# A chain of feed-forward and mixing layers on one core: the last group of the 512-token layers written out, with other buffers for activations and squares

## The chip, the cores and the metric

The kernel runs on one core of one Trainium2 chip. Its engines are TensorE (matmuls, PE in the profile), VectorE (DVE), ScalarE (ACT), GpSimd (POOL) and SyncE (SP), which issues most of the DMAs. The metric is the device time of one execution in microseconds; the kernel before has a median of 2832.19 us over 3 runs (2831.08 to 2836.46). A program order is given to each engine by hand, and engines wait for one another by semaphores; there is no scheduler.

## The reference, cut to what matters

The model has two blocks of two layers each over 256 tokens of width 1024; the first block also carries 256 context tokens along. Around every mixer (pooling, differential attention, a recurrent mixer, a dilated attention) stand gated feed-forward steps. All is in float32.

```python
def rms_norm(x, g):
    xf = x.astype(jnp.float32)
    y = xf * lax.rsqrt(jnp.mean(xf * xf, axis=-1, keepdims=True) + NORM_EPS)
    return (y * g.astype(jnp.float32)).astype(x.dtype)

def swiglu(h, w_in, w_out):
    g, u = jnp.split(h @ w_in, 2, axis=-1)
    return (jax.nn.silu(g) * u) @ w_out

def ffn_step(s, g, shift, scale, gate, w_in, w_out):
    return s + 0.5 * gate * swiglu(modulate(rms_norm(s, g), shift, scale), w_in, w_out)
...
x = ffn_step(x, ...)      # ffn 0 and, for layer 1, ffn 2: 256 tokens x and 256 tokens xc
x = x + mx[5] * ox        # ox: pooling in layer 0, attention in layer 1
x = ffn_step(x, ...)      # ffn 1 (with xc) and ffn 3 (x alone)
```

The hidden width is 2816, in 11 groups of 256. In the first block the modulation (`shift`, `scale`, `gate`) comes from two vectors times `ada_w`.

## The kernel before

**Layout.** Features lie on the partitions, tokens along a row: `x` is 128 x 8 x 512 (`KT` = 8 feature tiles; tokens 0 to 255 are `x`, 256 to 511 the context, `HALVES`). A matmul of two float32 operands is done as three (`mm3`): weights and activations are split into a high part (`whi`, `hh`, `ah`) and a low rest (`wlo`, `hl`, `al`). ScalarE makes each high part (`split_hi`), VectorE each low part (`split_lo`). Weights come in chunks of 1 MB into three slots of `wraw`; chunk n is split when the matmuls of chunk n - 3 are done.

**A feed-forward layer** (`ffn`, one such function for each engine). ffn 0, 1 and 2 have 512 tokens, ffn 3 to 7 have 256. For each of 11 groups: gate products into `ps_g`, up products into `ps_u`, ScalarE's silu into `sg`, VectorE's product into `tmp`, then the high part into `ah` (ScalarE, `hidden`) and the low rest into `al` (VectorE, `hidden`). TensorE's down products of a group run one group late: gate i+1, up i+1, down i. A down product has eight tiles, each in one of four PSUM banks `ps_o`; VectorE adds each into `x` (`residual`: two additions of 256 columns for 512 tokens) and thereby frees its bank (`o_free`). After the loop the down products of the last group follow at once. There is one `ah`/`al` for all groups. With 256 tokens the last iteration stands written out, and its activations go to the free half of the buffer (`last_hi`, `last_lo`), with VectorE's two splits placed among the tiles. With 512 tokens all ten iterations are in the loop. In ffn 0 to 2 VectorE also computes the modulation (`ada_block`, 3 or 4 a group, on rows loaded by GpSimd's queue), lines 1475 and 1478.

**A norm** (`norm`). ScalarE squares each tile of `x` after its last addition (line 765), GpSimd adds the first `POOLED[k]` squares up (line 668), TensorE multiplies the rest and the pooled sum with ones into `ps_g` (`pooled_sums`, line 2253), ScalarE takes roots (lines 784 and 786), VectorE the reciprocal (1296, 1291), and then each tile is scaled (VectorE, 1314), shifted into `hh` (ScalarE, 806) and its rest put in `hl` (VectorE, 1327), tokens 0 to 255 first. TensorE runs matmuls nobody reads meanwhile (`keep_clock`, 2237). The norms are numbered k: k = 1 stands between ffn 0 and the pool mixer, 2 ahead of ffn 1, 3 ahead of ffn 2, 4 ahead of the attention, k = 5 and on have 256 tokens. For k = 1 the whole 512 columns are handled in one piece, for 2 to 4 by halves from the root on.

**Late chunks.** The split of the chunk after the next two is put off to the end of the norm (`late`); for k = 4 `early=True` puts it ahead of the root and the reciprocal. There it is the chunk of the attention's v weights, the third of `qkv`. TensorE first makes two tiles of q and two of k (`diff_first`), then v tiles, each of which waits for the bank two tiles back. VectorE copies the q and k tiles out in order, behind the lambda arithmetic (lines 1778 to 1783).

## Time and profile before

| | us |
|---|---|
| median of 3 runs | 2832.19 |
| profiled execution, its own time | 2833.92 |
| its span | 2832.3 |
| TensorE busy | 2725.0 |
| VectorE busy | 2049.1 |
| ScalarE busy | 1011.9 |
| GpSimd busy | 139.6 |
| granted TensorE clock, mean | 0.981 |

A busy share says how long an engine had an instruction in it, not whether the end waited for it. A time line row gives start and duration in us, then engine, line and operation, with the idle time ahead of it and what ended it in brackets. Matmuls overlap: their pace is the distance of starts, not the duration shown. A line number is that of the kernel before.

### The profile page before, as it was taken

To read this page: it belongs to the slowest core of one execution; us is meant where nothing else is said; L and a number is where in the kernel's file an instruction comes from. 1 tells how busy PE (TensorE), PEld (TensorE's weight loads), DVE (VectorE), ACT (ScalarE), POOL (GpSimd) and SP (SyncE) were. 2 spreads that over 40 slices of the span, in tenths; PEclk is the share of its full clock that TensorE was granted. 3 is DMA by queue.
4 is the path that set the end of the run, shared out by engine and by line. 5 is a ranking of instruction groups with operands and counts; after the bars stand their busy time and mean duration, and the time that the engine had idled before them with its cause. 6 is when DMAs were issued, how large, how long until landed. Compare 5 with 4: busy or idle time off the path is not lost.

```text
span 2832.3 us, 49047 instructions
## 1 busy us (share of the span) xinstructions
PE 2725.0 (96%) x19250; PEld 2418.7 (85%) x19250; DVE 2049.1 (72%) x3067; ACT 1011.9 (36%) x1167; POOL 139.6 (5%) x204
## 2 busy tenths in 40 slices
PE   6999999999999999999999999998899999999999
PEld 4888878788878888788799899977799989986999
DVE  5877778766777777776676766756767776665677
ACT  4222234222232222333344444553144434443534
POOL 1000011000010000100000000000000010000000
PEclk9999999999999999999999999999999999997999
DMA  8444432533334444322245344521044554443344
GB/s 348 163 174 168 161 150 70 180 136 133 133 124 159 153 180 164 132 90 75 86 176 193 136 178 178 188 86 62 3 169 178 193 142 178 188 168 67 119 185 186
DMA packets 68705, 421.43 MB, mean 149 GB/s; under 512 B 7672, under 2 KB 8824, under 8 KB 26592
## 3 DMA queue, kind: packets, MB, share of 16 engines
q1 hardware_dynamic: 48176, 343.36, 32.8%
q0 software_dynamic: 20432, 76.69, 8.4%
q8 instruction: 71, 1.16, 0.2%
q14 instruction: 26, 0.21, 0.0%
HBM read 418.95 MB, written 1.07 MB: 148 GB/s over the span
## 4 chain that ended last, share of the span: by engine, by line
PE 84%; DVE 9%; issue 3%; ACT 2%; DMA 1%; POOL 1%; SPq 0%; DVEq 0%; ACTq 0%; POOLq 0%
PE ps_o L2230 11%; PE ps_o L2232 10%; PE ps_o L2231 10%; PE ps_g L2230 7%; PE ps_u L2230 7%; PE ps_u L2232 7%; PE ps_u L2231 7%; PE ps_g L2232 7%; PE ps_g L2231 7%; DVE wlo L1261 2%; PE ps_o L2469 1%; DMA scr<-in_AW 1%; DVE tsq L1314 1%; PE ps_g L2253 1%; DVE scr L1475 1%
## 5 line engine op out<-in xcount | busy, mean ns | idle before, releaser
L761 ACT ACTIVATE whi<-wraw 128x2048 fp32r<-128x2048 f32 x314 | 598.8, 1911 | 788.5 <-PE ps_u L2232 371.2
L1261 DVE TENSOR_TENSOR wlo<-wraw,whi 128x2048 fp32r<-128x2048 f32 x314 | 712.3, 2290 | 163.8 <-ACT whi L761 163.7
L2230 PE MATMUL ps_g<-hh,wlo 128*128 128x256 f32 (+1 forms) x1464 | 464.1, 317 | 6.4 <-DVE hl L1327 3.9
L2230 PE MATMUL ps_o<-ah,wlo 128*128 128x256 f32 (+1 forms) x1408 | 454.8, 323 | 15.5 <-DVE x L1367 7.9
L2230 PE MATMUL ps_u<-hh,wlo 128*128 128x256 f32 (+1 forms) x1464 | 462.5, 316 | 0.0
L2232 PE MATMUL ps_g<-hh,whi 128*128 128x256 f32 (+1 forms) x1464 | 462.1, 316 | 0.0
L2231 PE MATMUL ps_g<-hl,whi 128*128 128x256 f32 (+1 forms) x1464 | 462.1, 316 | 0.0
L2232 PE MATMUL ps_u<-hh,whi 128*128 128x256 f32 (+1 forms) x1464 | 462.1, 316 | 0.0
L2231 PE MATMUL ps_u<-hl,whi 128*128 128x256 f32 (+1 forms) x1464 | 461.9, 316 | 0.0
L2231 PE MATMUL ps_o<-al,whi 128*128 128x256 f32 (+1 forms) x1408 | 453.0, 322 | 0.0
L2232 PE MATMUL ps_o<-ah,whi 128*128 128x256 f32 (+1 forms) x1408 | 452.8, 322 | 0.0
L1367 DVE SCALAR_TENSOR_TENSOR x<-ps_o,gcol,x 128x256 f32<-128x256 f32 x640 | 281.9, 479 | 126.7 <-PE ps_o L2232 121.0
L2230 PEld LDWEIGHTS ps_g<-hh,wlo 128*128 128x128 f32 x1464 | 275.9, 188 | 29.6 <-issue 10.6
L2230 PEld LDWEIGHTS ps_o<-ah,wlo 128*128 128x128 f32 x1408 | 265.6, 189 | 40.3 <-issue 8.8
L2231 PEld LDWEIGHTS ps_g<-hl,whi 128*128 128x128 f32 x1464 | 275.9, 188 | 18.6
L2230 PEld LDWEIGHTS ps_u<-hh,wlo 128*128 128x128 f32 x1464 | 275.7, 188 | 18.9 <-issue 0.2
L2232 PEld LDWEIGHTS ps_g<-hh,whi 128*128 128x128 f32 x1464 | 275.8, 188 | 18.7
L2231 PEld LDWEIGHTS ps_u<-hl,whi 128*128 128x128 f32 x1464 | 275.7, 188 | 18.7
L2232 PEld LDWEIGHTS ps_u<-hh,whi 128*128 128x128 f32 x1464 | 275.7, 188 | 18.7
L2232 PEld LDWEIGHTS ps_o<-ah,whi 128*128 128x128 f32 x1408 | 265.8, 189 | 21.1
L2231 PEld LDWEIGHTS ps_o<-al,whi 128*128 128x128 f32 x1408 | 265.6, 189 | 20.8
L880 ACT ACTIVATE ah<-tsq 128x512 fp32r<-128x512 f32 (+1 forms) x88 | 69.8, 793 | 463.0 <-PE ps_o L2232 447.0
(461 smaller groups left out, 3677.0 us busy)
## 6 DMA issues: line engine op xcount, KB each, us to landing
wraw<-in_W SPq DMA_DIRECT2D x315, 1024.0 KB, 4.8
...
x<-in_XT SPq DMA_DIRECT2D x1, 2048.0 KB, 10.3
...
```

The lines of the kernel that those rows point to most:

```text
L761: nc.scalar.activation(whi[:, n % SLOTS, :], wraw[:, n % SLOTS, :], ACT.Copy).then_inc(w_hi, 1)
L880: nc.scalar.activation(dst[:, :, 0:N], tmp[:, :, 0:N], ACT.Copy).then_inc(a_hi, 1)
L1261: tt_(wlo[:, n % SLOTS, :], wraw[:, n % SLOTS, :], whi[:, n % SLOTS, :].bitcast(f32), sub).then_inc(w_lo, 1)
L1314: stt(dst, src(d)[:, HALVES[j]], A(d, j), rstd[:, HALVES[j]], mult, mult).then_inc(nm_t, 1)
L1367: ins = stt(x[:, d, HALVES[j]], src[:, HALVES[j]], gate(d, j), x[:, d, HALVES[j]], mult, add)
L1475: stt(ada_junk[:, 0, :], ada_w[:, slot, :], 1.0, ada_c[:, 0, :], mult, mult, accum_out=mod_col(b, 0, i, per)).then_inc(ad_left, 1)
L2230: mm(out, a[1], b[0], start=first, stop=False)
L2231: mm(out, a[0], b[1], start=False, stop=False)
L2232: return mm(out, a[0], b[0], start=False, stop=last)
L2253: ins = mm(out, ones, tsq[:, d * NTOK:d * NTOK + N], start=d == order[0], stop=d == order[-1])
L2469: ins = mm(att_out(g)[unit["rows"]], unit["v"][b], probs_t[a][g % 2][:, b, :], start=b == 0, stop=b == nb - 1)
```

## The change

The last iteration of the loop is written out for 512 tokens as well, on ScalarE and VectorE. Its activations go to new buffers `th` and `tl`, which lie in the second half of `tsq`; the squares 4 to 7 of the norms after these layers (k = 1, 3, 4: `AFTER_WIDE`) go to `hid` instead. For k = 2, 3, 4 (`SUM_HALVES`) each sum of squares is made of two matmuls of 256 columns in two banks, and the first half has a semaphore step of its own. `POOLED` is 5 in place of 6 for k = 1, 3, 4, and the pooled sum is taken as the last but one. The early split of k = 4 is gone. In the written-out iteration, for 256 tokens too, the second split stands behind two tiles of the last group instead of three.

```diff
 LATE = (5, 7)
-POOLED = {1: 6, 2: 6, 3: 6, 4: 6, 5: 4, 6: 4, 7: 3, 8: 6, 9: 6, 10: 6, 11: 6, 12: 6}
+SUM_HALVES = (2, 3, 4)
+AFTER_WIDE = (1, 3, 4)
+POOLED = {1: 5, 2: 6, 3: 5, 4: 5, 5: 4, 6: 4, 7: 3, 8: 6, 9: 6, 10: 6, 11: 6, 12: 6}
...
         x = sb("x", [128, KT, NTOK])
+        with nc.sbuf_tensor("off_t", [128, KT * NTOK // 2], f32), nc.sbuf_tensor("th", [128, 2, NTOK], f32r) as th, nc.sbuf_tensor("tl", [128, 2, NTOK], f32r) as tl:
+            pass
...
         wide, narrow = (hh, hl, ah, al), (hh2, hl2, ah2, al2)
-        last_hi, last_lo = ah2[:, :, NX:NTOK], al2[:, :, NX:NTOK]
+        last = {NX: (ah2[:, :, NX:NTOK], al2[:, :, NX:NTOK]), NTOK: (th, tl)}
...
             return [(b0 + q, s, fills[s] + slots[:q + 1].count(s)) for q, s in enumerate(slots)], fills
+        def squared_at(k, d, N):
+
+            return cut(hid, (d - KT // 2) * NTOK, N) if k in AFTER_WIDE and d >= KT // 2 else cut(tsq, d * NTOK, N)
+
+        def summed(k, part=1):
+
+            return k + sum(q < k for q in SUM_HALVES) + 1 + (part if k in SUM_HALVES else 0)
+
...
         HN_MEM = [ps_o[:, 3, :], BANK[3]]
-        ffn_loop = lambda N: GROUPS - 2 if N == NX else GROUPS - 1
+        ffn_loop = GROUPS - 2
...
                         pool.wait_ge(nm_acc, pooled(k) + d - 1)
-                    nt(tsq[:, 0:N], tsq[:, 0:N], tsq[:, d * NTOK:d * NTOK + N], add).then_inc(nm_acc, 1)
+                    nt(tsq[:, 0:N], tsq[:, 0:N], squared_at(k, d, N), add).then_inc(nm_acc, 1)
...
                 nc.scalar.activation(whi[:, n % SLOTS, :], wraw[:, n % SLOTS, :], ACT.Copy).then_inc(w_hi, 1)
-            def square(src, N, ready, d):
+            def square(src, N, ready, d, k=0):
                 ready(act, d)
-                nc.scalar.activation(tsq[:, d * NTOK:d * NTOK + N], src(d)[:, 0:N], ACT.Square).then_inc(nm_sq, 1)
+                nc.scalar.activation(squared_at(k, d, N), src(d)[:, 0:N], ACT.Square).then_inc(nm_sq, 1)
...
                     for d in range(squared, KT):
-                        square(src, N, ready, d)
+                        square(src, N, ready, d, k)
                         memory_out(memory, 0)
-                    act.wait_ge(nm_sum, k + 1)
+                    act.wait_ge(nm_sum, summed(k, 0))
                     rest = HALVES[1] if by_half else slice(0, N)
-                    nc.scalar.activation(rstd[:, rest], ps_g[:, 0, rest], ACT.Sqrt, bias=C("eps", 1), scale=1.0 / D).then_inc(nm_std, 1)
+                    act.wait_ge(nm_sum, summed(k))
+                    nc.scalar.activation(rstd[:, rest], ps_g[:, 1, 0:NX] if k in SUM_HALVES else ps_g[:, 0, rest], ACT.Sqrt, bias=C("eps", 1), scale=1.0 / D).then_inc(nm_std, 1)
...
                     split_hi(n0 + 7, i, step, per)
-                if N == NX:
-                    i = GROUPS - 2
-                    if f not in LATE:
-                        split_hi(n0 + 5, i, step, per)
-                    silu(i * step + DONE[n0 + 2], i + (g0 + 1), i + (lg + 2))
-                    if f in LATE:
-                        split_hi(n0 + 5, i, step, per)
-                    nc.scalar.activation(cols[:, 61:62], C("eps", 1), ACT.Sqrt)
-                    hidden(i + (g0 + 1), last_hi)
-                    split_hi(n0 + 6, i, step, per)
-                    split_hi(n0 + 7, i, step, per)
+                i = GROUPS - 2
+                if f not in LATE:
+                    split_hi(n0 + 5, i, step, per)
+                silu(i * step + DONE[n0 + 2], i + (g0 + 1), i + (lg + 2))
+                if f in LATE:
+                    split_hi(n0 + 5, i, step, per)
+                nc.scalar.activation(cols[:, 61:62], C("eps", 1), ACT.Sqrt)
+                hidden(i + (g0 + 1), last[N][0])
+                split_hi(n0 + 6, i, step, per)
+                split_hi(n0 + 7, i, step, per)
...
             ffn(2, NTOK)
-            norm(lambda d: x[:, d, :], NTOK, mod(1, 1), "split", after(FIRST["qkv", 0]), FIRST["qkv", 0], part=3, early=True)
+            norm(lambda d: x[:, d, :], NTOK, mod(1, 1), "split", after(FIRST["qkv", 0]), FIRST["qkv", 0], part=3)
...
                     split_lo(n_down + SLOTS, i, per)
-                if N == NX:
-                    i = GROUPS - 2
-                    done = i * step + DONE[n_down - 1]
-                    if f in LATE:
-                        scale_gate(i * step + DONE[n0 + 2], i + (g0 + 1))
-                        scale_silu(i + (g0 + 1))
+                i = GROUPS - 2
+                done = i * step + DONE[n_down - 1]
+                for s in range(per_ada):
+                    if s == 2:
+                        split_lo(n0 + 5, i, per)
+                    ada_block(b0 + s, s, 16 * (fills[s] + 1), i, per_ada)
+                if f in LATE:
+                    scale_gate(i * step + DONE[n0 + 2], i + (g0 + 1))
+                    scale_silu(i + (g0 + 1))
+                if per_ada < 3:
                     split_lo(n0 + 5, i, per)
-                    product(i + (g0 + 1), i * step + DONE[n_up], i + (lg + 2))
-                    down(n_down, done, range(1))
-                    hidden(i + (g0 + 1), last_hi, last_lo)
-                    down(n_down, done, range(1, 4))
-                    split_lo(n_up + SLOTS, i, per)
-                    down(n_down, done, range(4, KT))
-                    down(n_last, DONE[n_last - 1], range(3))
-                    split_lo(n_down + SLOTS, i, per)
-                    down(n_last, DONE[n_last - 1], range(3, KT))
-                else:
-                    down(n_last, DONE[n_last - 1])
+                product(i + (g0 + 1), i * step + DONE[n_up], i + (lg + 2))
+                down(n_down, done, range(1))
+                hidden(i + (g0 + 1), *last[N])
+                down(n_down, done, range(1, 4))
+                split_lo(n_up + SLOTS, i, per)
+                down(n_down, done, range(4, KT))
+                down(n_last, DONE[n_last - 1], range(2))
+                split_lo(n_down + SLOTS, i, per)
+                down(n_last, DONE[n_last - 1], range(2, KT))
...
             ffn(2, NTOK, gate(1, 0))
-            norm(xs_, NTOK, A_mod(1, 1), B_mod(1, 1), "split", part=3, early=True)
+            norm(xs_, NTOK, A_mod(1, 1), B_mod(1, 1), "split", part=3)
...
             def pooled_sums(out, k, N):
-                order = [0] + list(range(POOLED[k], KT))
-                if POOLED[k] == 4:
-                    order = [4, 5, 6, 0, 7]
-                elif POOLED[k] < 6:
+                order = [*range(POOLED[k], KT - 1), 0, KT - 1] if k < 7 else [0, *range(POOLED[k], KT)]
+                if k == 7:
                         pe.wait_ge(nm_sq, k * KT + d + 1)
-                    ins = mm(out, ones, tsq[:, d * NTOK:d * NTOK + N], start=d == order[0], stop=d == order[-1])
-                ins.then_inc(nm_sum, 1)
+                    if k in SUM_HALVES:
+                        for j, half in enumerate(HALVES):
+                            ins = mm(ps_g[:, j, 0:NX], ones, squared_at(k, d, N)[:, half], start=d == order[0], stop=d == order[-1])
+                            if d == order[-1]:
+                                ins.then_inc(nm_sum, 1)
+                    else:
+                        ins = mm(out, ones, squared_at(k, d, N), start=d == order[0], stop=d == order[-1])
+                if k not in SUM_HALVES:
+                    ins.then_inc(nm_sum, 1)
...
                     down(n_down, i * tiles + TILE0[n_down], i + g0, i)
-                down(n_last, TILE0[n_last], g0 + GROUPS - 1, last=f < 7, a=(last_hi, last_lo) if N == NX else (ah, al))
+                down(n_last, TILE0[n_last], g0 + GROUPS - 1, last=f < 7, a=last[N])
```

The helper for a source's place, and the number of steps of the sums' semaphore, are `squared_at` and `summed` above. What moves on three engines follows, before and after apart.

VectorE, end of ffn 0: from the loop's branch, before (`mods` and `acol` are modulation arithmetic):

```order
L1399 TENSOR_TENSOR al<-tsq,ah 128x1024
L1260 REGISTER_ALU
L1261 TENSOR_TENSOR wlo<-wraw,whi 128x2048
L1260 REGISTER_ALU
L1261 TENSOR_TENSOR wlo<-wraw,whi 128x2048
L1427 REGISTER_ALU
L1427 COMPARE_AND_BRANCH
L1367 SCALAR_TENSOR_TENSOR x<-ps_o,gcol,x 128x256 x16
L1527 TENSOR_TENSOR mods<-mods,vec 128x40 x2
```

The same place after, from the product of the last written-out group:

```order
L1407 TENSOR_TENSOR tsq<-tsq,ps_u 128x1024
L1379 SCALAR_TENSOR_TENSOR x<-ps_o,gcol,x 128x256 x2
L1411 TENSOR_TENSOR tl<-tsq,th 128x1024
L1379 SCALAR_TENSOR_TENSOR x<-ps_o,gcol,x 128x256 x6
L1273 TENSOR_TENSOR wlo<-wraw,whi 128x2048
L1379 SCALAR_TENSOR_TENSOR x<-ps_o,gcol,x 128x256 x12
L1273 TENSOR_TENSOR wlo<-wraw,whi 128x2048
L1379 SCALAR_TENSOR_TENSOR x<-ps_o,gcol,x 128x256 x12
L1541 TENSOR_TENSOR mods<-mods,vec 128x40 x2
```

The low rest comes behind one tile of the last but one group (two additions a tile), one split behind four tiles, the other behind two tiles of the last group.

TensorE, end of ffn 1 and the sums of squares of k = 3, before (`cst` holds the ones, `ps_u` is written by `keep_clock`):

```order
L2230 MATMUL ps_o<-ah,wlo 128x512
L2231 MATMUL ps_o<-al,whi 128x512
L2232 MATMUL ps_o<-ah,whi 128x512
L2253 MATMUL ps_g<-tsq,cst 128x512 x3
L2237 MATMUL ps_u<-cst 128x512 x4
```

And after:

```order
L2244 MATMUL ps_o<-th,wlo 128x512
L2245 MATMUL ps_o<-tl,whi 128x512
L2246 MATMUL ps_o<-th,whi 128x512
L2267 MATMUL ps_g<-hid,cst 128x256 x4
L2267 MATMUL ps_g<-tsq,cst 128x256 x2
L2267 MATMUL ps_g<-hid,cst 128x256 x2
L2251 MATMUL ps_u<-cst 128x512 x4
```

Three sums of 512 columns become eight of 256: squares 5 and 6, the pooled sum, square 7.

VectorE, end of the norm ahead of the attention, before (`hl` is the norm's last step, `lamb` the lambda arithmetic, `scr<-ps_o` the copies of q and k):

```order
L1327 SCALAR_TENSOR_TENSOR hl<-tsq,mods,hh 128x256 x2
L1778 TENSOR_TENSOR lamb<-lamb 128x64 x2
L1779 TENSOR_REDUCE cols<-lamb 128x2
L1781 TENSOR_TENSOR cols<-cols 128x1
L1782 TENSOR_SCALAR cols<-cols 128x1
L1783 TENSOR_SCALAR cols<-vec 128x1
L1662 TENSOR_SCALAR scr<-ps_o 128x256 x2
L1664 COPY scr<-ps_o 128x512 x2
```

And after:

```order
L1339 SCALAR_TENSOR_TENSOR hl<-tsq,mods,hh 128x256 x2
L1273 TENSOR_TENSOR wlo<-wraw,whi 128x2048
L1792 TENSOR_TENSOR lamb<-lamb 128x64 x2
L1793 TENSOR_REDUCE cols<-lamb 128x2
L1795 TENSOR_TENSOR cols<-cols 128x1
L1796 TENSOR_SCALAR cols<-cols 128x1
L1797 TENSOR_SCALAR cols<-vec 128x1
L1676 TENSOR_SCALAR scr<-ps_o 128x256 x2
L1678 COPY scr<-ps_o 128x512 x2
```

The split of the v weights stands ahead of the lambda arithmetic and of all copies; ScalarE's half of it moves behind the last tile of the norm in the same way.

## Rows read from the trace of the kernel before

**Rows 1.** The page: busy time, share of the span and instructions of TensorE.

```profile
PE 2725.0 (96%) x19250; PEld 2418.7 (85%) x19250; DVE 2049.1 (72%) x3067; ACT 1011.9 (36%) x1167; POOL 139.6 (5%) x204
```

**Rows 2.** Time line of TensorE, end of ffn 0: start, duration, instruction, idle before.

```profile
396.35 0.59 PE L2230 MATMUL ps_o<-ah,wlo 128*128 128x512 f32 x1 [2.53 <-issue]
...
408.70 0.39 PE L2232 MATMUL ps_o<-ah,whi 128*128 128x512 f32 x1
410.06 2.84 PE L2253 MATMUL ps_g<-tsq,cst 128*128 128x512 f32 x6 [0.97 <-POOL tsq L668]
```

**Rows 3.** Time line of ScalarE, end of ffn 0.

```profile
393.93 1.06 ACT L880 ACTIVATE ah<-tsq 128x1024 fp32r<-128x1024 f32 x1 [9.04 <-PE ps_o L2232]
...
410.04 0.63 ACT L765 ACTIVATE tsq<-x 128x512 f32<-128x512 f32 x1 [0.73 <-DVE x L1367]
```

**Rows 4.** Time line of VectorE, end of ffn 0.

```profile
383.15 1.22 DVE L1395 TENSOR_TENSOR tsq<-tsq,ps_u 128x1024 f32<-128x1024 f32 x1 [2.24 <-PE ps_u L2232]
...
393.85 0.88 DVE L1367 SCALAR_TENSOR_TENSOR x<-ps_o,gcol,x 128x256 f32<-128x256 f32 x2 [0.48 <-PE ps_o L2232]
395.02 1.23 DVE L1399 TENSOR_TENSOR al<-tsq,ah 128x1024 fp32r<-128x1024 f32 x1 [0.29 <-ACT ah L880]
396.16 4.48 DVE L1261 TENSOR_TENSOR wlo<-wraw,whi 128x2048 fp32r<-128x2048 f32 x2
```

**Rows 5.** Time line of GpSimd, end of ffn 0.

```profile
402.97 7.04 POOL L668 TENSOR_TENSOR tsq<-tsq 128x512 f32<-128x512 f32 x5 [15.97 <-ACT tsq L765]
```

**Rows 6.** Stretches: length, busy TensorE (x), loads, DVE, ACT, POOL; granted clock, DMA.

```profile
396.35:400.06 3.71, 3.71 (x9) 2.91 (x10) 3.71 (x2) 1.93 (x3) 0.00 (x0) 0.54 0.32 89
1182.40:1186.00 3.60, 3.60 (x16) 2.97 (x17) 3.60 (x2) 1.92 (x3) 0.00 (x0) 1.00 0.15 27
```

**Rows 7.** Time lines of ScalarE and VectorE, ends of ffn 1 and ffn 2.

```profile
806.96 1.06 ACT L880 ACTIVATE ah<-tsq 128x1024 fp32r<-128x1024 f32 x1 [9.04 <-PE ps_o L2232]
...
826.53 1.75 DVE L1296 RECIPROCAL rstd<-rstd 128x256 f32<-128x256 f32 x1 [2.86 <-ACT rstd L784]
...
1179.97 1.06 ACT L880 ACTIVATE ah<-tsq 128x1024 fp32r<-128x1024 f32 x1 [9.04 <-PE ps_o L2232]
...
1196.96 2.29 DVE L1261 TENSOR_TENSOR wlo<-wraw,whi 128x2048 fp32r<-128x2048 f32 x1 [2.50 <-ACT whi L761]
...
1200.27 1.75 DVE L1296 RECIPROCAL rstd<-rstd 128x256 f32<-128x256 f32 x1
```

**Rows 8.** Time lines of GpSimd, ScalarE and TensorE ahead of ffn 1 (k = 2).

```profile
438.06 6.95 POOL L668 TENSOR_TENSOR tsq<-tsq 128x512 f32<-128x512 f32 x5 [28.05 <-ACT tsq L765]
...
444.09 0.63 ACT L765 ACTIVATE tsq<-x 128x512 f32<-128x512 f32 x1 [0.15 <-DVE x L1367]
...
445.07 2.84 PE L2253 MATMUL ps_g<-tsq,cst 128*128 128x512 f32 x6 [2.04 <-POOL tsq L668]
```

**Rows 9.** Time lines of ScalarE, VectorE and TensorE, start of the attention.

```profile
1216.19 0.51 ACT L806 ACTIVATE hh<-tsq,mods 128x256 fp32r<-128x256 f32 x1 [0.28 <-DVE tsq L1314]
...
1217.14 0.48 DVE L1778 TENSOR_TENSOR lamb<-lamb 128x64 f32<-128x64 f32 x2
...
1218.82 0.76 DVE L1662 TENSOR_SCALAR scr<-ps_o 128x256 f32<-128x256 f32 x2
1221.01 1.29 DVE L1664 COPY scr<-ps_o 128x512 f32<-128x512 f32 x2 [1.44 <-PE ps_o L2232]
...
1221.85 0.36 PE L2230 MATMUL ps_o<-whi,hl 128*128 128x256 f32 x1 [0.52 <-DVE scr L1664]
```

**Rows 10.** Time lines of VectorE, GpSimd and TensorE, end of ffn 4.

```profile
1803.99 0.42 DVE L1367 SCALAR_TENSOR_TENSOR x<-ps_o,x 128x256 f32<-128x256 f32 x1 [0.28 <-PE ps_o L2232]
1804.33 2.80 DVE L1261 TENSOR_TENSOR wlo<-wraw,whi 128x2048 fp32r<-128x2048 f32 x1
...
1804.25 3.47 POOL L668 TENSOR_TENSOR tsq<-tsq 128x256 f32<-128x256 f32 x2 [191.27 <-ACT tsq L765]
...
1807.52 0.39 PE L2230 MATMUL ps_o<-ah,wlo 128*128 128x256 f32 x1 [0.77 <-DVE x L1367]
```

6 lines of the change are left out of this document (3 added, 3 removed).

## The prediction, made before the changed kernel ran

> **What bounds the kernel now.** I read the engines' shares first. TensorE is busy for 2725.0 of 2832.3 us [rows 1], so a change pays only where TensorE stands still, or where the whole core waits for a normalisation between two layers. Then I read the time line engine by engine at the end of the three 512-token feed-forward layers (ffn 0, 1, 2), and there both happen. I count from T0, the moment at which the products of the last but one group are finished and ScalarE may write `ah`: 393.93, 806.96 and 1179.97 us [rows 3, 7].
>
> At T0 of ffn 0 TensorE has nothing to do: its next matmul starts at 396.35, 2.53 us later [rows 2], because `ah` (1.06 us, ScalarE) and then `al` (1.23 us, VectorE, at 395.02) are written into the buffer that the products before have only just left [rows 3, 4]. VectorE then still has two weight splits to do, 4.48 us in one piece [rows 4], so the residual additions come late, the squares too, and GpSimd starts its five additions only at 402.97 and needs 7.04 us [rows 5]. They end at 410.01; TensorE's three 512-column sums start at 410.06 and take 2.84 us [rows 2]. The sums thus end 19.0 us after T0. The last matmul of the layer started at 408.70: it was the chain residual, square, GpSimd that set the end, not the matmuls. The granted clock agrees: after the stall of ffn 0 it was 0.54 for 3.7 us (1.2 GHz), after that of ffn 2 it was 1.00 (2.4 GHz) [rows 6], yet reciprocals start 19.57 us after T0 in ffn 1 and 20.30 in ffn 2 [rows 7], where an extra split stands ahead of it. What the clock took in one of them was hidden under GpSimd.
>
> **The last iteration written out, `th`/`tl` (ffn 0 to 2).** The last group's activations get their own place, so they can be written as soon as the gated product is there (383.15 + 1.22 = 384.4 [rows 4]), 9 us ahead of T0. ScalarE's table load goes ahead of it into idle time: ScalarE had waited 9.04 us [rows 3]. TensorE then runs on. A tile of six matmuls of 512 columns comes every 0.88 + 0.48 = 1.36 us [rows 4], so one takes 0.227 (16 in 3.60 us at full clock [rows 6]). VectorE takes up the last tile at 393.85, so the next matmul could start at about T0 - 0.3, and 48 of them end at about T0 + 10.6.
> Is VectorE fast enough? A tile's two additions take 0.88 us and leave 0.48 us to spare [rows 4]. Ahead of T0 it gets `tl` (1.23) after tile 0 and one split (4.48 / 2 = 2.24) after tile 3: it comes back to its tiles about 2 us late and is level again after four or five of them. By my count the four PSUM banks never hold up TensorE: the last layer's first tile needs tile 4 of the group before, added by T0 - 1.5. The second split comes after tile 1 of the last group, T0 + 3.5 to 5.75; the next tiles are added at 6.6, 7.4, 8.25, 9.1, 10.3 and 11.7. Squares (0.63 us each [rows 3]) follow 0.65 us behind, the last at T0 + 12.35.
> GpSimd now has four additions of 1.4 us (7.04 / 5 [rows 5]). The first waits for the split to leave (below), T0 + 5.8 to 7.1, the fourth ends at T0 + 11.5. TensorE sums squares 5 and 6 first, from T0 + 10.7, then the pooled sum, then square 7: four of 2.84 / 3 = 0.95 us, ending at T0 + 14.45. Every input is there about 1 us before it is wanted. Gain: 19.0 - 14.45 = **4.55 us** in ffn 0. One sum more on TensorE (0.95) is in it.
>
> **Sums by halves** (before ffn 1, ffn 2 and the attention). Each sum becomes two of 256 columns, 0.47 us each, and ScalarE's first root needs only the first. That is 0.47 us earlier; the second half's root and reciprocal stand behind the first half's sixteen VectorE instructions in the order. In ffn 1: 4.55 + 0.47 = **5.0 us**.
>
> **Before ffn 1**, after the pool mixer, GpSimd keeps five additions (6.95 us from 438.06) and square 7 is ready at 444.09 + 0.63 [rows 8]. TensorE's three sums start at 445.07. Now square 6 is summed ahead of the pooled sum, while TensorE waits. Saved: 0.95 + 0.47 = **1.4 us**.
>
> **Before the attention.** Today a split stands at 1196.96 ahead of modulation arithmetic and of the reciprocal at 1200.27, 20.30 after T0 [rows 7]. Moved behind the norm, it frees the reciprocal to start with the sums: the first root's input at T0 + 13.95, the root 0.47, reciprocal at T0 + 14.45. Gain 5.85. But that split is the v weights'. It now comes when ScalarE has finished the norm's last unit (1216.19 + 0.51), 1.90 on ScalarE, 2.20 on VectorE: until 1220.8 on the present time line. Queued behind it on VectorE are the lambda arithmetic, 1.68 us (1217.14 to 1218.82), two copies of q, 0.76, and the first copy of k, 0.69: 1223.9 instead of 1221.01 + 0.69 = 1221.7 [rows 9]. TensorE's first v tile, 1221.85 today, waits for exactly that bank: 2.2 us later. TensorE is then idle for nearly 3 us; after the earlier 2.5 us stalls the following matmuls cost 3.71 - 9 x 0.227 = 1.7 us extra (ffn 0) or nothing (ffn 2) [rows 6]. I take the middle, 0.9. Net: 5.85 - 2.2 - 0.9 = **2.7 us**.
> The Trainium skill ("TensorE: Matmul & The Clock Gate", Part 1) says the gate throttles an array that has been idle and that where the slow matmuls fall varies from run to run. By it both rows can be right; neither end is excluded.
>
> **Two tiles instead of three** ahead of the last split in the five 256-token layers. In ffn 4 tile 2 is added at 1803.99, the split runs from 1804.33 for 2.80 us, beside GpSimd's two additions of together 3.47, and TensorE's tile 7 starts at 1807.52, after 0.77 us of waiting [rows 10]. A tile comes every 0.42 + 0.28 = 0.70 us there. With the split one tile earlier, tile 1 is added by 1803.7, ahead of GpSimd's 1804.25, the split takes 2.24 to 1805.95, tile 2 is added by 1806.35; and now it is tile 6 that waits for this bank. It starts at 1806.4 and takes about 0.95 (0.39 for the first matmul, five of 0.115), tile 7 follows at 1807.35: 0.2 gained. Where there is no such collision (I count three of the five layers) the same sum gives 0.3 lost. Net: 3 x 0.3 - 2 x 0.2 = 0.5 lost, with -1.5 to +2 as bounds (five times a 0.3 to 0.4 us restart). I take **0.4 us lost**.
>
> **The sum.** 4.55 + 5.0 + 1.4 + 2.7 - 0.4 = 13.3 us. The profiled execution took 2833.92 (span 2832.3, the rest around it), 1.7 above the median of 2832.19. 2832.3 - 13.3 = 2819.0 of span; median to median 2832.2 - 13.3 = **2818.9 us**.
>
> **Rivals.**
> B, the late split is free: if copies and banks leave TensorE running, 3.1 us come back: 2815.8. For it: VectorE is idle for a while after the k copies. Against it: the bank wait is in today's profile (0.52 us idle) and VectorE's queue is in order. 0.12.
> C, GpSimd is the new bound. Its additions collide with VectorE instructions: in ffn 4 two took 3.47 us and the split beside them 2.80 [rows 10]. Against it: beside residual additions in ffn 0 five ran in 7.04 us without a stretch [rows 5]. One addition held until the split ends does no harm; if a second is held, or the squares come 2 us later than I count, the pooled sum is late by about 1.2 us in each of the three layers: 3.6 us less, 2822.5. 0.16.
> The Trainium skill ("SBUF — State Buffer", the section on two separate sides) makes it an exclusive lock, held for a whole instruction, between GpSimd and VectorE instructions with two SBUF inputs. Both rows agree with it: the split has two such inputs, a residual addition has one from PSUM. By the rule the sum stays as it is.
> D, the stall stays, for instance because the last group's weights are not split in time. Then only the rest acts: 1.4 + 2 x 0.47 + 0.85 - 3.1 - 0.4, about -0.3: 2832.5. Against it: that split stands ahead of the product of 383.15 in VectorE's order [rows 4], 10 us before T0. 0.06.
> E, slower: the new TensorE wait ahead of the v tile throws the clock to 1.2 GHz and it stays there. It decides when about 14 us of full-speed matmuls (five v tiles of 24 matmuls of 256 columns, half of 0.227 each) run at half speed; with 20 us of them the kernel needs 2838. Against it: after every stall I read the clock was back within 3.7 us. 0.04.
>
> **How the numbers follow.** My case 0.62 (alone 2816.5 to 2821.5: the clock term 0 to 1.7, the tile term, and 1 us of median noise), B 0.12, C 0.16, D 0.06, E 0.04. A difference of 0.2%, 5.7 us, is about what a measurement can tell from none. Faster: A + B + C = 0.90; same 0.06; slower 0.04. Range 2814.5 to 2825.5: it leaves out D and E and some of the far ends of B and C.
>
> **What would show it.** At the ends of ffn 0, 1 and 2: no idle time of TensorE between the two last groups, and GpSimd's additions over before the first sum; first root 14.0 to 14.5 us after T0 instead of 19.0. Before the attention: reciprocal directly after the root, one split after the norm, TensorE idle some 3 us ahead of its first v tile. In ffn 4: a split of 2.25 us, and tile 6 waiting. I am wrong if TensorE waits for banks in the last groups, if GpSimd's additions stretch, or if the clock stays low after the attention's wait.

## The result, and the profile after

| | before | after |
|---|---|---|
| median | 2832.19 us (5 runs, 2828.94 to 2836.46) | 2816.30 us (5 runs, 2808.51 to 2819.48) |
| ratio after/before | | 0.9938, 95% interval 0.9919 to 0.9958 |
| profiled execution, span | 2832.3 us | 2814.6 us |
| mean granted clock | 0.981 | 0.984 |

The changed kernel is 15.9 us faster by the medians; 13.3 was forecast (2818.9 us), and the range held the time. In a second comparison (below) it stood at 2814.97 against 2831.5.

The page after, busy times:

```profile
PE 2715.9 (96%) x19278; PEld 2417.4 (86%) x19278; DVE 2047.4 (73%) x3067; ACT 1012.0 (36%) x1170; POOL 138.5 (5%) x201
```

TensorE does 28 instructions more than in [rows 1] and is busy for 9.1 us less. Part of that is the clock: at full clock 16 matmuls took 3.60 us, at half clock 9 took 3.71 [rows 6]. How much of the 9.1 us it makes was not worked out.

End of ffn 0, where T0 is 393.80 us, the start of ScalarE's split here. First ScalarE: the early high part, T0, and the norm's root.

```profile
384.11 1.06 ACT L893 ACTIVATE th<-tsq 128x1024 fp32r<-128x1024 f32 x1 [7.74 <-DVE tsq L1407]
...
393.80 1.92 ACT L773 ACTIVATE whi<-wraw 128x2048 fp32r<-128x2048 f32 x1 [6.82 <-PE ps_o L2246]
...
408.11 0.69 ACT L799 ACTIVATE rstd<-ps_g,cst 128x512 f32<-128x512 f32 x1 [1.95 <-PE ps_g L2271]
```

`th` is written 9.7 us ahead of T0, where `ah` in [rows 3] came at T0, and the root starts at T0 + 14.31. VectorE's two splits, now apart from each other:

```profile
389.09 2.28 DVE L1273 TENSOR_TENSOR wlo<-wraw,whi 128x2048 fp32r<-128x2048 f32 x1
...
397.25 2.28 DVE L1273 TENSOR_TENSOR wlo<-wraw,whi 128x2048 fp32r<-128x2048 f32 x1
```

GpSimd's four additions of the same norm:

```profile
398.08 2.60 POOL L680 TENSOR_TENSOR tsq<-tsq 128x512 f32<-128x512 f32 x1 [11.16 <-ACT tsq L777]
401.06 2.74 POOL L680 TENSOR_TENSOR tsq<-tsq 128x512 f32<-128x512 f32 x2 [0.38 <-ACT tsq L777]
403.94 1.28 POOL L680 TENSOR_TENSOR tsq<-tsq,hid 128x512 f32<-128x512 f32 x1
```

TensorE: first tile of the last group, then the four sums.

```profile
393.54 0.39 PE L2244 MATMUL ps_o<-th,wlo 128*128 128x512 f32 x1
...
404.42 1.88 PE L2271 MATMUL ps_g<-hid,cst 128*128 128x512 f32 x4
406.13 1.02 PE L2271 MATMUL ps_g<-tsq,cst 128*128 128x512 f32 x2
406.99 1.02 PE L2271 MATMUL ps_g<-hid,cst 128*128 128x512 f32 x2
```

No bracket, so no idle time ahead of the last group, in contrast to the 2.53 us of [rows 2]. The sums follow one another without a wait and end at about T0 + 14.2. GpSimd was over at 405.22, 0.9 us before its sum was wanted. (Each sum counts as two in "x", as the three of [rows 2] did.)

Ahead of the attention: TensorE's sums by halves, then VectorE's reciprocal and late split, then TensorE's first v tile. T0 is 1168.73 us.

```profile
1179.36 1.89 PE L2267 MATMUL ps_g<-hid,cst 128*128 128x256 f32 x8
1181.08 1.03 PE L2267 MATMUL ps_g<-tsq,cst 128*128 128x256 f32 x4
```

```profile
1183.15 1.75 DVE L1308 RECIPROCAL rstd<-rstd 128x256 f32<-128x256 f32 x1 [1.75 <-ACT rstd L796]
...
1201.43 2.29 DVE L1273 TENSOR_TENSOR wlo<-wraw,whi 128x2048 fp32r<-128x2048 f32 x1 [1.32 <-ACT whi L773]
```

```profile
1206.78 0.36 PE L2244 MATMUL ps_o<-whi,hl 128*128 128x256 f32 x1 [2.56 <-DVE scr L1678]
```

The reciprocal starts 14.42 us after T0 ([rows 7]: 20.30). In [rows 9] the v tile waited 0.52 us, now 2.56. The stretch behind that wait (length, busy TensorE, loads, DVE, ACT, POOL, granted clock, DMA):

```profile
1206.70:1210.70 4.00, 3.92 (x22) 3.95 (x23) 0.53 (x1) 1.58 (x1) 0.00 (x0) 0.62 0.98 356
```

Half clock for most of 4 us, as predicted in kind.

**By stages.** The times between the starts of VectorE's reciprocals cut the program into stages. They are taken from the rows `RECIPROCAL rstd<-rstd` of each trace; "to k = 5" runs through the attention, "rest" from there to the end of the span. The first 36 us, up to the first reciprocal, are in no column.

| profiled execution | to k=1 | to k=2 | to k=3 | to k=4 | to k=5 | sum | rest |
|---|---|---|---|---|---|---|---|
| before | 377.54 | 34.73 | 378.08 | 373.73 | 211.24 | 1375.32 | 1420.75 |
| after | 372.83 | 33.45 | 372.95 | 367.86 | 214.43 | 1361.52 | 1417.02 |
| change | -4.71 | -1.28 | -5.13 | -5.87 | +3.19 | -13.80 | -3.73 |
| predicted | -4.55 | -1.4 | -5.0 | -5.85 | +3.1 | -13.7 | +0.4 |

In the stages that the change touches most, every term is met within 0.2 us, against this one profile of before. What was not forecast stands in the last column.

### The profile page after: what moved, and what is told of

The parts are those of the page before. It is cut to its first block, busy times and chain, and to the rows that moved or that the text cites. A ratio compares the mean times of both kernels' runs of the same rounds, so it can differ in the third digit from the quotient of the medians.

```text
span 2814.6 us, 49017 instructions
## 1 busy us (share of the span) xinstructions
PE 2715.9 (96%) x19278; PEld 2417.4 (86%) x19278; DVE 2047.4 (73%) x3067; ACT 1012.0 (36%) x1170; POOL 138.5 (5%) x201
## 4 chain that ended last, share of the span: by engine, by line
PE 85%; DVE 10%; issue 2%; ACT 2%; DMA 1%; SPq 0%; DVEq 0%; ACTq 0%
PE ps_o L2244 11%; PE ps_o L2245 10%; PE ps_o L2246 10%; PE ps_g L2244 7%; PE ps_u L2244 7%; PE ps_u L2245 7%; PE ps_u L2246 7%; PE ps_g L2245 7%; PE ps_g L2246 7%; DVE wlo L1273 2%; DVE tsq L1326 1%; PE ps_o L2488 1%; DMA scr<-in_AW 1%; DVE hl L1339 1%; DVE scr L1489 1%
## 5 line engine op out<-in xcount | busy, mean ns | idle before, releaser
L2244 PE MATMUL ps_o<-ah,wlo 128*128 128x256 f32 (+1 forms) x1360 | 434.7, 320 | 8.3 <-DVE x L1379 8.3
L2245 PE MATMUL ps_o<-al,whi 128*128 128x256 f32 (+1 forms) x1360 | 433.6, 319 | 0.0
L2246 PE MATMUL ps_o<-ah,whi 128*128 128x256 f32 (+1 forms) x1360 | 432.6, 318 | 0.0
L2244 PEld LDWEIGHTS ps_o<-ah,wlo 128*128 128x128 f32 x1360 | 255.7, 188 | 29.8 <-DVE x L1379 8.1
L2246 PEld LDWEIGHTS ps_o<-ah,whi 128*128 128x128 f32 x1360 | 256.0, 188 | 19.0
L2245 PEld LDWEIGHTS ps_o<-al,whi 128*128 128x128 f32 x1360 | 255.9, 188 | 18.8
## 6 DMA issues: line engine op xcount, KB each, us to landing
big<-in_AW SPq DMA_DIRECT2D x4, 1024.0 KB, 15.1
```

The source lines that it names most:

```text
L2244: mm(out, a[1], b[0], start=first, stop=False)
L2245: mm(out, a[0], b[1], start=False, stop=False)
L2246: return mm(out, a[0], b[0], start=False, stop=last)
```

## The experiments

Experiments 1 to 8 are one execution each, so they are read at the places that they change and not by their totals. Only the last two were timed several times.

**1 and 2. The same two kernels once more.** No edit. The question was whether the 4 us gained behind the attention belong to the change.

> The kernel before once more, for its trace. Theory A (the gain past the attention is chance): its stages after the attention differ from its first trace by some us in either direction, as the two kernels' do (4.7 us between the start of the attention and the end), though not one instruction differs. Theory B (the change acts there too, by the split's new place among the tiles): they agree within 0.5 us. Up to the attention both expect agreement within 1 us, but for the clock after the stalls of the 512-token layers.

> The changed kernel once more, for its trace. Both theories: first roots of the norms behind ffn 0, 1 and 2 about 14.3, 13.85 and 13.85 us after T0 as in its first trace. At the attention TensorE waits 2.56 us again; if the slow matmuls behind it are chance, its first v tile takes 2.9 us this time or 4.4 again. Theory A: the stages after the attention differ from the first trace by 1 to 4 us; theory B: within 0.5 us.

Measured: 2836.88 and 2820.08 us. The stages, with a third profile of the changed kernel from experiment 9:

| profiled execution | to k=1 | to k=2 | to k=3 | to k=4 | to k=5 | sum | rest |
|---|---|---|---|---|---|---|---|
| before_again | 377.49 | 36.27 | 378.10 | 375.09 | 210.75 | 1377.71 | 1421.71 |
| after_again | 372.82 | 33.46 | 371.34 | 367.84 | 215.79 | 1361.25 | 1420.90 |
| after_timed | 372.83 | 33.44 | 372.89 | 367.83 | 214.44 | 1361.44 | 1425.74 |

The rest of one and the same program takes 1417.0, 1420.9 and 1425.7 us, and their mean, 1421.2, is that of the two profiles of before (1420.75, 1421.71). Theory B, agreement within 0.5 us, is refuted. Six profiles of the experiments below have the changed kernel's code from the reciprocal of k = 5 on (same_home, whole_sums, six_pooled, early_split, fill_wait, mid_split): 1414.9 to 1419.2 us. The mean of all nine is 1418.4, 2.8 us below before. 1.0 us of that is the new place of the split (experiment 4); the remaining 1.8 us are small beside a spread of 10.8 us, so they are not shown to belong to the change.

Two components of the spread can be named. From the distances of VectorE's products: in a 256-token layer the iterations have one of two lengths, 16.76 to 16.81 or 16.94 to 16.97 us, and keep it for the whole layer; in ffn 5 it is 16.97 in the first profile of after and 16.81 in the third. That is 1.6 us a layer. The other is the granted clock in the stage with the recurrent mixer, which takes 270.4 to 277.5 us over the twelve profiles. Its shortest (fill_wait) and its longest (same_home), with the granted clock as the last but two of the numbers:

```profile
1798.76:2069.17 270.41, 247.90 (x3524) 213.87 (x3523) 184.30 (x403) 98.75 (x193) 6.22 (x8) 0.97 0.20 73
1807.61:2085.11 277.50, 256.03 (x3524) 221.60 (x3523) 184.34 (x404) 98.87 (x193) 6.24 (x8) 0.93 0.20 71
```

VectorE and ScalarE are busy for the same time in both; TensorE is busy for 8.1 us more where the clock was lower. What makes the clock fall more often there in one execution than in another, no run shows.

The touched stages vary too. In the changed kernel "to k=1", "to k=2" and "to k=4" repeat within 0.03 us. "To k=3" was once 1.6 us shorter (in after the granted clock was 0.51 from 501.2 to 504.6 us, in after_again it was 1.00 throughout) and "to k=5" once 1.4 us longer; that the sums agree within 0.3 us is partly these two cancelling. The kernel before varies by 1.5 us in "to k=2" and 1.4 us in "to k=4". Two rows of before_again on TensorE, the sums ahead of ffn 1 and the attention's first q tile:

```profile
444.52 4.40 PE L2253 MATMUL ps_g<-tsq,cst 128*128 128x512 f32 x6 [2.03 <-POOL tsq L668]
...
1206.22 0.36 PE L2230 MATMUL ps_o<-hh,wlo 128*128 128x256 f32 x1 [2.83 <-DVE hl L1327]
```

```profile
1206.10:1210.10 4.00, 3.88 (x20) 3.91 (x21) 4.00 (x11) 2.47 (x5) 0.00 (x0) 0.59 0.00 0
```

In [rows 8] the same sums after the same wait of 2.04 took 2.84 us; here 4.40, at half clock: the 1.5 us by which "to k=2" is longer. In the changed order TensorE waits only 0.97 us there, and "to k=2" is 33.44 to 33.46 us in all eight profiles that have that order and the halves.

At the end of ffn 2, before_again had the granted clock at 0.63 in the 4 us from 1183.43, behind its stall, where before had 1.00 [rows 6]. The sums on TensorE, and on ScalarE the split of the v weights behind the last square, first in before (T0 is 1179.97 us), then in before_again (T0 is 1181.02 us):

```profile
1196.06 2.84 PE L2253 MATMUL ps_g<-tsq,cst 128*128 128x512 f32 x6 [2.50 <-POOL tsq L668]
...
1195.04 1.89 ACT L761 ACTIVATE whi<-wraw 128x2048 fp32r<-128x2048 f32 x1
```

```profile
1197.11 2.84 PE L2253 MATMUL ps_g<-tsq,cst 128*128 128x512 f32 x6 [1.17 <-POOL tsq L668]
...
1197.42 1.89 ACT L761 ACTIVATE whi<-wraw 128x2048 fp32r<-128x2048 f32 x1
```

The sums start 16.09 us after T0 in both profiles, so GpSimd hid the slow clock from them. But ScalarE's split starts 1.33 us later than in before (16.40 against 15.07 us after T0), because the last tile and its square are late, and behind it come VectorE's split and the reciprocal: 1.4 us. At the end of ffn 0 no split stands ahead of the reciprocal, and there the cost was hidden: "to k=1" is 377.54 us with half clock (before) and 377.49 at full clock (before_again, 1.00 in the 4 us from 396.00).

**3. `th`/`tl` given up** (same_home). All the rest of the change stays: the written-out iteration, the places of the splits, five squares, halves. The activations go back to `ah`/`al` and their two writes behind the products of the group before:

```diff
-AFTER_WIDE = (1, 3, 4)
+AFTER_WIDE = ()
...
-        last = {NX: (...), NTOK: (th, tl)}
+        last = {NX: (...), NTOK: (ah, al)}
...
+                if N == NTOK:
+                    split_hi(n0 + 6, i, step, per)
+                    act.wait_ge(mm_done, i * step + DONE[n_down])
                 hidden(i + (g0 + 1), last[N][0])
...
                 down(n_down, done, range(4, KT))
+                if N == NTOK:
+                    hidden(i + (g0 + 1), *last[N])
```

> The last iteration of the 512-token layers written out, but its activations in the old ah/al, so that ScalarE waits for the last products but one and the squares stay in tsq. Theory A (the new place removes the wait of TensorE, the written-out order brings the squares forward): the stall of 2.5 us is back, with it 0 or 1.7 us of slow clock; the last matmul ends 13.1 to 14.8 us after T0 instead of 10.6, the first root comes 17 to 18.5 us after T0 where the changed kernel has 14 and the kernel before 19. Theory B (the place alone brings the gain): 19.0 again. Theory C (the order alone): 14 to 14.5. In all, A expects 8 to 12 us more than the changed kernel.

Measured: 2828.11 us. ScalarE's write of `ah`, which is T0, and the first root, at the ends of ffn 0, 1 and 2:

```profile
392.63 1.06 ACT L893 ACTIVATE ah<-tsq 128x1024 fp32r<-128x1024 f32 x1 [8.90 <-PE ps_o L2253]
...
411.33 0.69 ACT L799 ACTIVATE rstd<-ps_g,cst 128x512 f32<-128x512 f32 x1 [1.95 <-PE ps_g L2278]
...
804.01 1.06 ACT L893 ACTIVATE ah<-tsq 128x1024 fp32r<-128x1024 f32 x1 [8.90 <-PE ps_o L2253]
...
820.65 0.47 ACT L796 ACTIVATE rstd<-ps_g,cst 128x256 f32<-128x256 f32 x1 [1.48 <-PE ps_g L2274]
...
1174.59 1.06 ACT L893 ACTIVATE ah<-tsq 128x1024 fp32r<-128x1024 f32 x1 [8.90 <-PE ps_o L2253]
...
1192.74 0.47 ACT L796 ACTIVATE rstd<-ps_g,cst 128x256 f32<-128x256 f32 x1 [1.48 <-PE ps_g L2274]
```

TensorE's first matmul after the stall of ffn 2, and the 4 us behind each of the three stalls:

```profile
1177.00 0.77 PE L2251 MATMUL ps_o<-ah,wlo 128*128 128x512 f32 x1 [2.45 <-issue]
```

```profile
395.04:399.04 4.00, 4.00 (x11) 3.17 (x12) 0.88 (x2) 0.78 (x3) 0.00 (x0) 0.57 0.78 317
806.43:810.43 4.00, 4.00 (x18) 3.29 (x19) 1.84 (x5) 1.22 (x4) 0.00 (x0) 1.00 0.02 4
1177.00:1181.00 4.00, 4.00 (x11) 3.19 (x12) 0.88 (x2) 0.68 (x3) 0.00 (x0) 0.60 0.00 0
```

Theory A holds in kind: TensorE's stall is back, and the three stages together are 11.3 us longer, within its 8 to 12. Two of the three roots miss its 17 to 18.5 us. Roots at T0 + 18.70, 16.64 and 18.15, against 14.31 at the end of ffn 0 and 13.85 at that of ffn 2 in the changed kernel. By stages the buffers are worth 4.34, 2.70 and 4.23 us. The clock tells why the middle one is smaller: where it stayed at 1.00, only the stall of 2.45 us counts; where it was 0.57 to 0.60, another 1.5 to 1.6 us. Against before, the rest of the edits had brought only 0.4 us in the first stage (377.17 against 377.54), where stall and slow clock now set the end. In the second they brought 2.4 us, with the clock at 1.00 and 0.4 us of halves in it; in the third, with the late split, 1.6 us. `th` and `tl` without the reordering were not run.

**4. Three tiles ahead of the last split, in the 256-token layers** (three_tiles).

```diff
-                down(n_last, DONE[n_last - 1], range(2))
+                down(n_last, DONE[n_last - 1], range(2 if N == NTOK else 3))
                 split_lo(n_down + SLOTS, i, per)
-                down(n_last, DONE[n_last - 1], range(2, KT))
+                down(n_last, DONE[n_last - 1], range(2 if N == NTOK else 3, KT))
```

> The changed kernel with three tiles ahead of the last split in the 256-token layers, as in the kernel before. Theory A (the prediction's sum): ffn 4 and ffn 6 0.2 us longer, ffn 3, 5 and 7 0.3 us shorter than in the changed kernel, in each from the last product's addition to the first tile of the next stage; the whole within 0.5 us but for chance. Theory B (the place is the source of the gain past the attention): ffn 3 to 7 together 3 to 4 us longer.

Measured: 2823.85 us. From the last gated product to the end of the last residual addition, ffn 3 to 7: 13.07, 13.32, 12.80, 13.33, 12.80 us with three tiles and 13.05, 12.80, 12.80, 12.81, 12.81 with two. Two tiles gain 0.52 us in ffn 4 and ffn 6, nothing in the others, 1.0 in all. Both theories are refuted: A forecast 0.2 us in ffn 4 and 6, with the right sign, and 0.3 us the other way in the other three, where nothing changed; B wanted 3 to 4 us. End of ffn 4 with three tiles, on GpSimd, VectorE and TensorE:

```profile
1791.61 3.47 POOL L680 TENSOR_TENSOR tsq<-tsq 128x256 f32<-128x256 f32 x2 [190.72 <-ACT tsq L777]
```

```profile
1791.70 2.80 DVE L1273 TENSOR_TENSOR wlo<-wraw,whi 128x2048 fp32r<-128x2048 f32 x1
```

```profile
1794.89 0.39 PE L2244 MATMUL ps_o<-ah,wlo 128*128 128x256 f32 x1 [0.77 <-DVE x L1379]
```

and with two, in the changed kernel:

```profile
1790.61 2.25 POOL L680 TENSOR_TENSOR tsq<-tsq 128x256 f32<-128x256 f32 x1 [189.77 <-ACT tsq L777]
```

```profile
1789.99 2.28 DVE L1273 TENSOR_TENSOR wlo<-wraw,whi 128x2048 fp32r<-128x2048 f32 x1
```

```profile
1792.66 0.39 PE L2244 MATMUL ps_o<-ah,wlo 128*128 128x256 f32 x1 [0.25 <-DVE x L1379]
```

Whoever starts first goes through, and the other waits for it. Started ahead of GpSimd's addition, the split takes 2.28 instead of 2.80, and the addition pays (2.25 us, of which 0.6 lie behind the split's end), which nobody waits for. The wait that I had expected at tile 6 is there, but 0.25 us and not 0.5 to 0.6. In the layers without a collision it is there as well, and with three tiles the same wait stands ahead of tile 7. Ffn 3, with three tiles and then with two:

```profile
1588.32 0.39 PE L2244 MATMUL ps_o<-ah,wlo 128*128 128x256 f32 x1 [0.35 <-DVE x L1379]
```

```profile
1587.69 0.38 PE L2244 MATMUL ps_o<-ah,wlo 128*128 128x256 f32 x1 [0.35 <-DVE x L1379]
```

The wait only moves by a tile; that is why nothing is lost or gained there. In ffn 5 and 7 it is 0.23 to 0.25 us in either order.

The Trainium skill ("SBUF — State Buffer", the section on two separate sides) makes the shared port an exclusive lock, and the rows agree: in ffn 0 the addition beside the split took 2.60 us, where the next two together took 2.74.

**5. Sums in one piece** (whole_sums).

```diff
-SUM_HALVES = (2, 3, 4)
+SUM_HALVES = ()
```

> The sums of squares ahead of the norms at k = 2, 3 and 4 are made in one piece over all 512 tokens again; k = 1 keeps what it has. Theory A (my term of 0.47 us each, 1.4 us in all: the last pair of TensorE's sums lies on the path ahead of the root): the first root of the norms at k = 2, 3 and 4 comes 0.4 to 0.6 us later after the last moment products than in the changed kernel, and the shift of VectorE's reciprocals against the changed kernel grows by that much at each of the three, 1.2 to 1.7 us by the start of the attention. Theory B (the second half of the norm, not the first, sets the end): the first root is later, but the shift at the next landmark behind the norm is under 0.2 us each.

Measured: 2820.68 us. From the end of the last gated product to the reciprocal: 24.55 us against 24.13 at k = 3 and at k = 4; "to k=2" 33.86 against 33.45; and the first v tile keeps it (48.16 against 47.76). The halves are worth 0.41 us in each of three norms, 1.2 in all; my 0.47 was 0.06 too much. It was 2.84 / 6, and the 2.84 us hold the end of the last matmul once; the starts of the halves stand 0.43 us apart (four from 1179.36 to 1181.08 us, above). Theory A holds.

**6. Six pooled squares** (six_pooled), and three at k = 2 with the old order of the sums.

```diff
-POOLED = {1: 5, 2: 6, 3: 5, 4: 5, ...}
+POOLED = {1: 6, 2: 6, 3: 6, 4: 6, ...}
...
+                if k == 2:
+                    order = [0, 6, 7]
```

The second edit alone acts at k = 2, where `POOLED` was 6 in either kernel: the sum of square 6 stands behind the pooled one again. What was expected on record speaks of two and three additions there; the number of additions at k = 2 doesn't change, only the order does.

> GpSimd makes six squares' additions instead of five at the ends of ffn 0, ffn 1 and ffn 2, and three instead of two at k = 2. Theory A (the number of additions is what frees the end of the iteration): GpSimd's chain ends 1.3 us later; at the ends of ffn 0 to 2 that puts it behind ScalarE's last square, and the first root comes 0.2 to 0.6 us later than the 14.4 us after the last moment products that the changed kernel has; at k = 2 about 0.9 us later. Theory B (GpSimd's own chain isn't near the path, VectorE's last tile is): no change at the ends of ffn 0 to 2 (within 0.1 us).

Measured: 2818.15 us. GpSimd's last additions and TensorE's pooled sum, end of ffn 2:

```profile
1181.36 2.69 POOL L680 TENSOR_TENSOR tsq<-tsq,hid 128x512 f32<-128x512 f32 x2
```

```profile
1184.10 1.13 PE L2269 MATMUL ps_g<-tsq,cst 128*128 128x256 f32 x4 [0.70 <-POOL tsq L680]
```

TensorE waits 0.70 us for the fifth addition. The reciprocals come 0.66, 0.66 and 0.65 us later at k = 1, 3 and 4, and 0.87 at k = 2. So in the changed kernel GpSimd is off the path by less than an addition, and theory A holds in kind (its 0.2 to 0.6 us were a little low); one addition less on GpSimd, in exchange for one sum more on TensorE, is worth 0.65 us a norm.

**7. The early split put back** (early_split).

```diff
-            norm(..., "split", after(FIRST["qkv", 0]), FIRST["qkv", 0], part=3)
+            norm(..., "split", after(FIRST["qkv", 0]), FIRST["qkv", 0], part=3, early=True)
...
-            norm(xs_, NTOK, A_mod(1, 1), B_mod(1, 1), "split", part=3)
+            norm(xs_, NTOK, A_mod(1, 1), B_mod(1, 1), "split", part=3, early=True)
```

> The splits of the attention's v weights are put back in front of the norm before the attention, on ScalarE and VectorE, everything else as in the changed kernel. Theory A (my two terms: 3 us won ahead of the norm, 3 to 3.6 us lost again ahead of the first v tile): the first reciprocal of that norm comes 3.0 to 3.4 us later after the last moment products (17.4 to 17.8 us against 14.4), TensorE doesn't wait ahead of the first v tile (under 0.3 us) and runs it at full clock, and the first v tile starts within 0.7 us of where it does in the changed kernel. Theory B (the split in front of the norm is hidden behind VectorE's last tile): the reciprocal comes under 1 us later, and the first v tile over 2 us earlier than in the changed kernel, so that the whole kernel is faster than the changed one by over 2 us at that place.

Measured: 2815.71 us. Reciprocal 3.08 us later, as A said, and B is refuted. The first v tile however starts 2.53 us later than in the changed kernel, not within 0.7, and waits 0.52 us, not under 0.3. TensorE, first q tile and first v tile, and the 4 us behind the start of the q tile:

```profile
1189.77 0.36 PE L2244 MATMUL ps_o<-hh,wlo 128*128 128x256 f32 x1 [3.39 <-DVE hl L1339]
...
1209.29 0.36 PE L2244 MATMUL ps_o<-whi,hl 128*128 128x256 f32 x1 [0.52 <-DVE scr L1678]
```

```profile
1189.77:1193.77 4.00, 4.00 (x21) 4.00 (x22) 4.00 (x11) 2.54 (x5) 0.00 (x0) 0.57 0.00 0
```

It runs at full clock (1.00 in the 4 us from 1209.30). But the split ahead of the norm outlasts the matmuls that nobody reads, so TensorE idles for 3.39 us ahead of the q tiles (0.31 in the same place without it), and the clock is low there instead. At the attention's first scores the early split is 1.02 us behind the late one (58.28 against 57.26 us from the last gated product), of which the slow q tiles are 1.5. At the reciprocal of k = 5 the two are level (238.64 and 238.57 us). The late split thus costs what it brings within about 1 us: the 2.7 net of the prediction come from the other parts of the change, and the choice between the two is a choice of which wait TensorE has.

**8. Matmuls in the wait** (fill_wait).

```diff
                 diff_first()
+                keep_clock(2, BANK[3])
                 n = FIRST["qkv", 0] + 2
```

> Ahead of the first v tile of the attention, while TensorE waits for the late split, it is given dummy matmuls (the kernel's keep_clock), whose result nobody reads. Theory A (the wait costs twice, once by itself and once by the clock that is low behind it): the v tile still starts 2 to 2.6 us after TensorE's last real matmul, but takes 2.9 to 3.1 us instead of 4.4, and the start of the attention is 1.3 to 1.6 us earlier than in the changed kernel. Theory B (the tile is slow for another reason, the weights' or the transposes' path): it takes 4.2 us or more as before, and nothing is won.

Measured: 2813.54 us. TensorE's fill and the first v tile, and the 4 us from there:

```profile
1204.11 1.88 PE L2251 MATMUL ps_u<-cst 128*128 128x512 f32 x4
1206.82 0.35 PE L2244 MATMUL ps_o<-whi,hl 128*128 128x256 f32 x1 [0.84 <-DVE scr L1678]
```

```profile
1206.82:1210.82 4.00, 4.00 (x27) 3.51 (x28) 0.88 (x2) 1.50 (x1) 0.00 (x0) 1.00 1.00 353
```

The tile starts at the same time and takes 2.95 us instead of 4.44; the first scores come 1.51 us earlier, the reciprocal of k = 5 1.52. So theory A: the wait costs once by itself and, as a rule, once by the clock. How much by the clock varies, and the fill was run once. From the start of the first v tile to that of the second it is 4.75 us here and in mid_split, 6.0 to 6.25 in five profiles with the same wait (after, after_timed, same_home, three_tiles, whole_sums), 7.5 in after_again, and 4.75 in six_pooled, which waited 2.56 us as well and then had full clock:

```profile
1209.90 0.36 PE L2244 MATMUL ps_o<-whi,hl 128*128 128x256 f32 x1 [2.56 <-DVE scr L1678]
```

```profile
1209.90:1213.90 4.00, 4.00 (x27) 3.51 (x28) 0.88 (x2) 1.50 (x1) 0.00 (x0) 1.00 0.96 357
```

That is 1.3 to 1.5 us in five of seven executions, 0 in one and 2.8 in one. Full clock behind one filled wait could therefore be luck too, though less likely.

**9 and 10. A better place for the split** (mid_split), timed beside the changed kernel (after_timed, no edit). ScalarE's part goes between the norm's two halves, where ScalarE is ahead; VectorE's part then needn't wait for it; and the lambda arithmetic goes behind the k copies.

```diff
+                    if k == 4 and not again and (d, j) == (0, 1):
+                        split_hi(st["late"].pop())
...
+                        if (c, j) == (0, 1):
+                            lambdas()
```

> The changed kernel itself, for comparison with the version beside it. Every stage up to the attention ends within 1 us of the first profile of it; the total is 14 to 18 us below the kernel before, and differs by a few us from run to run.

> ScalarE's part of the v split is made between the two halves of the norm before the attention, VectorE's part at the norm's end, and the arithmetic for lambda is moved behind the first k copies. Theory A (the late split costs 3.6 us because VectorE's part waits for ScalarE's and stands ahead of the q and k copies): the norm's first reciprocal stays 14.4 us after the last moment products, TensorE's wait ahead of the first v tile falls from 2.05 us to under 0.5, the v tile takes 2.9 to 3.1 us instead of 4.4, and the start of the attention is 3 to 3.6 us earlier than in the changed kernel. Theory B (another step of the norm's end, the copies or the transposes, is late next): the wait ahead of the v tile stays over 1.2 us, and less than 1.5 us is won. In the total 3 us are near what five runs can tell.

Measured: before 2831.50 us (median of 11 runs, 2825.93 to 2839.63), after_timed 2814.97 (6 runs, 2809.3 to 2823.51), ratio 0.9936 (0.992 to 0.9953); mid_split 2811.18 (6 runs, 2802.39 to 2819.89), ratio 0.9925 (0.9904 to 0.9945). What was expected of after_timed came true: every stage up to the attention within 0.1 us of the first profile, and 16.5 us below before. The intervals of the two versions overlap, so the total doesn't settle which is faster, but the place does. ScalarE's part, VectorE's part and k copies, TensorE's first v tile:

```profile
1191.92 1.90 ACT L773 ACTIVATE whi<-wraw 128x2048 fp32r<-128x2048 f32 x1
```

```profile
1200.58 2.28 DVE L1275 TENSOR_TENSOR wlo<-wraw,whi 128x2048 fp32r<-128x2048 f32 x1
...
1204.45 1.29 DVE L1690 COPY scr<-ps_o 128x512 f32<-128x512 f32 x2 [0.92 <-PE ps_o L2253]
```

```profile
1205.28 0.36 PE L2251 MATMUL ps_o<-whi,hl 128*128 128x256 f32 x1 [0.52 <-DVE scr L1690]
```

VectorE now waits 0.92 us for TensorE ahead of the k copies, so the split is wholly hidden. The reciprocal stays where it was (24.13), the v tile starts 2.04 us earlier, waits 0.52 as in the kernel before, and runs at full clock; the first scores come 3.54 us earlier, "to k=5" is 4.26 us shorter. Theory A holds, but for 0.02 us of the wait. At this place the version is 3.5 us faster than the changed kernel; the medians are 3.8 us apart, which these runs can't tell from chance.

## Why the prediction was right

**The end of ffn 0 and 1.** The sum went through the cover of each step (products, tiles, splits, squares, additions, sums) and each stood within 0.3 us of where it was put: GpSimd's first addition held until the split ended (398.08 to 400.68, T0 + 6.9; predicted 7.1), sums from T0 + 10.6 (10.7), root at 14.31 and 13.85. The four sums come every 0.86 us and not every 0.95, which is most of what they end early by. Of rival C (GpSimd as the new bound) the condition didn't come: one addition was held, as in my own case, and the second started after the split. Six_pooled shows how near it was, 0.65 us for one addition more.

**What the stall cost.** I took the slow clock behind TensorE's stall as hidden under GpSimd. For the sums of squares that is right: at the end of ffn 0 half and full clock differ by 0.05 us in "to k=1", and at the end of ffn 2 the sums start at the same 16.09 us after T0. It is not right for the path through the early split at the end of ffn 2, which starts behind the last square: there before_again was 1.4 us slower than the profile on record. The forecast of 5.85 us matched 5.87 because that profile had full clock at this place; that is luck. In same_home, where GpSimd no longer hides it, the slow clock cost 1.5 to 1.6 us.

**The attention.** Forecast 3.1 us lost behind the reciprocal, measured 3.19 to k = 5 and 3.54 at the place (2.04 of wait and 1.5 of clock). The wait of 2.2 was sized well; for the clock I took the middle of 0 and 1.7, and it was 1.3 to 1.5 in most executions. What I did not see is the other side of the same edit: the early split made TensorE idle ahead of the q tiles (1.49 us in before, 2.83 in before_again, 3.39 in experiment 7), with a slow clock in two of the three. Rival E is refuted: after the v tile's start the clock was back within 4.5 us in all profiles but one, and there within 7. Rivals B and D are refuted as well: the v tile waited 2.56 us, and TensorE's stall was gone.

**Two tiles instead of three.** The one step with the wrong sign: forecast 0.4 us lost, measured 1.0 gained. Two terms of it failed. With the split one tile earlier, tile 6 waits 0.25 us in ffn 4 and not 0.5 to 0.6, so 0.52 us are gained there and not 0.2. And for the three layers without a collision I charged 0.3 us each for the wait of tile 6, as if there were none with three tiles; but tile 7 waited then, for as long (0.35 us in ffn 3), and nothing is lost.

**Where the other 2.6 to 3.2 us are.** Median to median the change brought 15.9 and 16.5 us in the two comparisons, 13.3 forecast. Of the difference 1.4 is the two-tile term. The touched stages of before may hold another 1 to 2: with its second profile their mean is 1376.5 us, against 1361.4 in the three of after, 15.1 instead of 13.8. Two and three profiles are few, and one and the same kernel ranges over 14 us in its total (2809.3 to 2823.51), so beyond the two-tile term this is plausible, not shown.
